# Fused two-block kernel: heads in pairs, a score group moved, a norm applied to results, a tile in another bank

## The chip, the cores and the metric

The kernel runs on one core of a Trainium2 chip. The metric is device time in microseconds (us), from the launch of the program to its end. PE is TensorE, DVE is VectorE, ACT is ScalarE, POOL is GpSimd, SP is SyncE, which issues most DMAs.

## What is computed

512 tokens of width 1024 pass two layers of a first block and one layer of a second, all in float32. Cut to what matters:

```python
for i in range(2):                                   # first block
    q_na, k_na, v_na, q_r, k_r, v_r, g_r, gate_a, gate_b = split(x @ w_in[i])
    ya = neighbourhood_attention(q_na, k_na, v_na, na_rpb[i])   # 8 heads of 64, 8x16 windows on an 8x64 grid
    yb = silu(g_r) * norm(retention(q_r, k_r, v_r))             # 4 heads, both directions
    y = (sigmoid(gate_a) * (ya @ w_branch_a) + sigmoid(gate_b) * (yb @ w_branch_b)) @ w_out[i]
    x = layer_norm(ALPHA * x + y)
    ffn = conv_glu_ffn(x); ple = sigmoid(x @ w_ple_gate) * (p[i] @ w_ple_proj)
    x = layer_norm(ALPHA * x + ffn + ple)
u = rmsnorm(h) @ w_in_2                              # second block
h = h + concat(pool_mixer(u[:, :512]), ssm_mixer(u[:, 512:])) @ w_out_2
h = h + (silu(rmsnorm(h) @ w_gate) * (rmsnorm(h) @ w_up)) @ w_down
out = rmsnorm(h)                                     # rmsnorm(x) = x / rms(x) * g
```

## The kernel before

Activations lie feature-major: `z`, `xh` and `xl` hold 8 tiles of 128 features by 512 tokens. Each float32 operand of a large product is split into a rounded part (`_hi`, float32r) and a remainder (`_lo`), and `passes` issues three products (hi*hi, lo*hi, hi*lo) in place of one.

Weights stream through a ring of four slots in *units* of 8 tiles of 128x128. SP loads a unit into `stage`, ACT rounds it to `w_hi` (L1184, `round_ahead`, three units ahead), POOL subtracts to `w_lo` (L419). PE takes a unit when `lo_done` says so. `feature_unit` runs 8 x 3 products of 512 columns into one of two unit banks, `U_BANK[0]` and `U_BANK[1]`, which alternate by the number of the result; `take_bank` waits until the reader of the result two before has freed it.

The order of each engine is written out by hand; engines meet in semaphores. One attention iteration, four in each layer, handles two neighbourhood heads and one retention head with 12 units. On PE: units 0 and 1 (q, k of the neighbourhood), 2 (v), scores and the transposes of v (`turn_v`), 3 (retention q), scores, transposes of the first probabilities (`turn_probs`), scores, 4 (retention k, the fifth unit), then probability-value products (`pv`), transposes and the two *token units* 5 and 6 in turn. A token unit writes results 5 and 6: its first half goes to bank 1, whose last reader is DVE's `rotate(0)`, its second half to bank 0, whose last reader is `rotate(1)` (L1622, L1623). Score tile i has head i // 4 and column block i % 4, lies in `S_BANK[i % 2]`, and is 256 or 384 columns wide. On DVE the order is: bias and mask of head 0 (`mask_scores(0)`, L1587, L1595, closing with the negation L1604), `normalise(0)` (L1615) behind ACT's four exps (L1214), `mask_scores(1)`, `rotate(0)`, `normalise(1)`, `rotate(1)`, then low parts for retention. The four retention score tiles (m = 0 to 3) also go through `S_BANK[m % 2]`, and DVE applies the decay (L1665).

After attention come the branches, whose merged result DVE writes at L1740, and the output projection of 8 units. For each of its results DVE runs `residual_out`: z = ALPHA*xh + result (L1751, frees the bank), z = ALPHA*xl + z (L1754); between the first and second it forms `p_lo` (L1749). POOL sums z tiles for the mean (L629).

In the mixer (second block) the output products `half_units(MS_U0...)` add to z, ACT squares each tile, POOL sums six of the squares (L629), PE forms the mean square (L947), ACT the root, DVE the reciprocal, PE spreads it over partitions (L962), and `rms` on DVE with `rms_split` on ACT writes the normed tile, its rounded part and its remainder (L1870, L1377, L1863). Only then `first_units` starts the gate and up products, whose loop handles four units a turn: ACT applies silu to the gate's bank, DVE multiplies by the up bank (`hidden`).

Of the kernel before, what the change touches and what calls it, by code (L numbers as in the profile page):

```python
# [18 lines left out]
P = 128  # L19
T = 512  # L20
# [73 lines left out]
def build(nc, a, out):  # L94

    ctx = ExitStack()
    with ctx:
# [143 lines left out]
        xn_2 = [place(f"xn_2{i}", [P, T], offset=c_at + 2048 * i) for i in range(4)]  # L241
# [4 lines left out]
        silu = [place(f"silu{i}", [P, T], offset=c_at + 2048 * i) for i in range(2)]  # L246
        hidden = [place(f"hidden{i}", [P, T], offset=c_at + 4096 + 2048 * i) for i in range(2)]
# [47 lines left out]
        z_ready, mean_done, centred = sem("z_ready"), sem("mean_done"), sem("centred")  # L295
# [25 lines left out]
        mix_hi_s, mix_lo_s = sem("mix_hi"), sem("mix_lo")  # L321
        gu_hi, gu_lo = sem("hidden_hi"), sem("hidden_lo")
# [32 lines left out]
        def _(sp):  # L355
# [53 lines left out]
            for first in range(0, KT, 2):  # L409
                sp.wait_ge(normed, (MIX * 2 + 1) * KT + (first + 2))  # L410
                sp.dma_start(out[:, first:first + 2, :], out_t[:, first:first + 2, :]).then_inc(out_done, 16)
# [4 lines left out]
        def _(pool):  # L416
# [216 lines left out]
            for L in range(DEPTH):  # L633
# [6 lines left out]
                for k in range(KT):  # L640
                    low_part(base + OUT0 // RING + 1 + k // RING, k % RING)
                    if 1 <= k < KT - 1:
                        add_tile(z_sum, z_tile, k, z_summed, 2 * L * (KT - 2), (z_ready, L * KT + (k + 1)))
# [102 lines left out]
        def _(pe):  # L746
# [28 lines left out]
            def first_units(L, u, r, x_done, ui=0, ri=0, parts=x_parts):  # L775
# [4 lines left out]
                for k in range(KT + lag):  # L780
                    for i in range(2):
# [29 lines left out]
            def attention(L, t):  # L811
# [7 lines left out]
                def scores(hh, js):  # L819
                    for r in range(2):  # L820
                        pe.wait_ge(*after_result(L, r, ri))
                    r0 = hh * NA_DH
                    q, k = ([v[r0:r0 + NA_DH, :] for v in parts] for parts in ((na_q, na_lo[0]), (na_k, na_lo[1])))
                    for j in js:
                        dst = take_score(4 * hh + j)
                        bs = kblocks(j)
                        keys = slice((j - 1 + bs[0]) * P, (j + bs[-1]) * P)
                        passes(dst[:, bs[0] * P:(bs[-1] + 1) * P], [v[:, j * P:(j + 1) * P] for v in q], [v[:, keys] for v in k],
                               True, True).then_inc(score_done, 1)
# [9 lines left out]
                def turn_probs(i):  # L839
                    j = i % CB  # L840
# [9 lines left out]
                def pv(i):  # L850
                    hh, j = i // CB, i % CB
                    if i == 0:
                        pe.wait_ge(o_norm, it * 4 + 4)
                        pe.wait_ge(v_ready, it + 1)
                    pe.wait_ge(pt_ready, it * 8 + (i + 1))
                    r0 = hh * NA_DH
                    dst = Y_BANK[r0:r0 + NA_DH, j * P:(j + 1) * P]
# [8 lines left out]
                scores(0, (0, 1))  # L866
                turn_v()
                scores(0, (2, 3))
# [11 lines left out]
                pv(2)  # L880
                pv(3)
# [3 lines left out]
                pv(4)  # L885
                pv(5)
# [3 lines left out]
                for m in range(4):  # L890
                    dst = take_score(8 + m)
# [3 lines left out]
                pv(6)  # L895
                pv(7)
# [76 lines left out]
            def out_proj(L):  # L973
# [6 lines left out]
                mean(L * 2, (z_ready, L * KT + KT))  # L980
# [58 lines left out]
            def mixer():  # L1039
# [110 lines left out]
                mean_square(n0 + 1, rstd_2, sq_2[(KT - 1) % 4])  # L1150
                spread(n0 + 1, rstd_2)
# [1136 lines left out]
```

## Time and profile before

| | us |
|---|---|
| median of 3 runs | 2444.66 |
| lowest and highest | 2443.77, 2446.43 |
| profiled execution | 2447.06 |
| its span, first to last instruction | 2445.3 |
| PE busy in it | 2366.5 (97%) |
| DVE, ACT, POOL busy | 957.5, 977.6, 1117.3 |

Times in rows count from the start of the span. A row of a timeline is a start, a duration, an engine, a line of the kernel, an operation, output and inputs with shapes, how many were merged, and in brackets the idle time of the engine ahead of it and what ended that. A PE row's duration includes the way through the array, so products overlap; their rate is read from their starts. The granted clock is a share of 2.4 GHz.

### The profile page before, as it was taken

To read this page: it belongs to the slowest core of one execution; us is meant where nothing else is said; L and a number is where in the kernel's file an instruction comes from. 1 tells how busy PE (TensorE), PEld (TensorE's weight loads), DVE (VectorE), ACT (ScalarE), POOL (GpSimd) and SP (SyncE) were. 2 spreads that over 40 slices of the span, in tenths; PEclk is the share of its full clock that TensorE was granted. 3 is DMA by queue.
4 is the path that set the end of the run, shared out by engine and by line. 5 is a ranking of instruction groups with operands and counts; after the bars stand their busy time and mean duration, and the time that the engine had idled before them with its cause. 6 is when DMAs were issued, how large, how long until landed. Compare 5 with 4: busy or idle time off the path is not lost.

```text
span 2445.3 us, 32512 instructions
## 1 busy us (share of the span) xinstructions
PE 2366.5 (97%) x11792; PEld 1947.1 (80%) x11792; DVE 957.5 (39%) x1490; ACT 977.6 (40%) x1320; POOL 1117.3 (46%) x684
## 2 busy tenths in 40 slices
PE   7999999999999998999999999999999889999998
PEld 6877888878888886888888877888887667888886
DVE  6454453343434203553553234434465594111101
ACT  4343343243555414433434225455522424444321
POOL 5677333445344453333333454344454664444442
PEclk9999999999999998999999999999999899999999
DMA  5212223213332332222222322222333112332331
GB/s 185 76 51 75 84 69 95 95 61 108 98 95 93 129 97 65 79 77 73 77 68 68 111 95 79 94 92 96 103 104 103 53 35 78 99 97 88 102 101 54
DMA packets 61136, 214.14 MB, mean 88 GB/s; under 512 B 7184, under 2 KB 7440, under 8 KB 61072
## 3 DMA queue, kind: packets, MB, share of 16 engines
q1 hardware_dynamic: 58624, 205.91, 26.3%
q10 hardware_dynamic: 2448, 7.34, 0.9%
q8 instruction: 44, 0.72, 0.1%
q14 instruction: 20, 0.16, 0.0%
HBM read 211.13 MB, written 2.10 MB: 87 GB/s over the span
## 4 chain that ended last, share of the span: by engine, by line
PE 89%; DVE 6%; ACT 2%; issue 2%; POOL 1%; SPq 0%; DMA 0%; DVEq 0%; ACTq 0%; POOLq 0%
PE psum L750 84%; PE psum L860 2%; DVE s_t L1615 1%; DVE states L1968 1%; PE psum L847 1%; ACT s_t L1214 1%; PE psum L947 1%; ACT z L1340 0%; DVE z L1762 0%; ACT xh L1339 0%; PE psum L962 0%; DMA convp<-in_convp 0%; PE psum L1063 0%; POOL rstd L629 0%; POOL w_lo L419 0%
## 5 line engine op out<-in xcount | busy, mean ns | idle before, releaser
L419 POOL TENSOR_TENSOR w_lo<-stage,w_hi 128x1024 fp32r<-128x1024 f32 x378 | 920.5, 2444 | 1261.6 <-ACT w_hi L1184 1247.0
L750 PE MATMUL psum<-xh,w_hi 128*128 128x512 f32 x1888 | 746.9, 396 | 17.5 <-DVE xl L2101 9.6
L750 PE MATMUL psum<-xl,w_hi 128*128 128x512 f32 x1888 | 741.4, 393 | 0.0
L750 PE MATMUL psum<-xh,w_lo 128*128 128x512 f32 x1888 | 741.0, 392 | 0.0
L1184 ACT ACTIVATE w_hi<-stage 128x1024 fp32r<-128x1024 f32 x377 | 396.6, 1053 | 354.0 <-PE psum L750 352.4
L750 PEld LDWEIGHTS psum<-xh,w_hi 128*128 128x128 f32 x1888 | 358.5, 190 | 100.3 <-issue 14.9
L750 PEld LDWEIGHTS psum<-xh,w_lo 128*128 128x128 f32 x1888 | 358.3, 190 | 75.9
L750 PEld LDWEIGHTS psum<-xl,w_hi 128*128 128x128 f32 x1888 | 358.8, 190 | 72.9
L750 PE MATMUL psum<-g_hi,w_hi 128*128 128x512 f32 x528 | 205.4, 389 | 0.0
L750 PE MATMUL psum<-g_lo,w_hi 128*128 128x512 f32 x528 | 205.4, 389 | 0.0
L750 PE MATMUL psum<-g_hi,w_lo 128*128 128x512 f32 x528 | 205.4, 389 | 0.0
L750 PEld LDWEIGHTS psum<-g_lo,w_hi 128*128 128x128 f32 x528 | 99.1, 188 | 20.6
L750 PEld LDWEIGHTS psum<-g_hi,w_hi 128*128 128x128 f32 x528 | 99.1, 188 | 20.6
L750 PEld LDWEIGHTS psum<-g_hi,w_lo 128*128 128x128 f32 x528 | 99.1, 188 | 20.5
L1365 ACT ACTIVATE conv_b<-psum,convp 128x512 f32<-128x512 f32 x44 | 34.3, 779 | 145.6 <-PE psum L750 145.6
L1817 DVE SCALAR_TENSOR_TENSOR conv_b<-psum,convp,conv_b 128x511 f32<-128x511 f32 x44 | 33.0, 750 | 149.3 <-ACT conv_b L1365 149.3
L2066 DVE TENSOR_TENSOR hidden<-psum,silu 128x512 f32<-128x512 f32 x22 | 15.2, 692 | 183.6 <-PE psum L750 183.6
L750 PE MATMUL psum<-w_hi,xh 128*128 128x256 f32 x256 | 74.6, 291 | 4.6 <-DVE r_tmp L1623 4.6
L750 PE MATMUL psum<-merged_p,w_hi 128*128 128x512 f32 x256 | 78.8, 389 | 0.0
L750 PE MATMUL psum<-w_lo,xh 128*128 128x256 f32 x256 | 73.1, 285 | 0.0
L750 PE MATMUL psum<-w_hi,xl 128*128 128x256 f32 x256 | 73.1, 285 | 0.0
L1839 DVE TENSOR_TENSOR z<-z,psum 128x512 f32<-128x512 f32 x16 | 11.0, 687 | 152.0 <-PE psum L750 152.0
(361 smaller groups left out, 3258.6 us busy)
## 6 DMA issues: line engine op xcount, KB each, us to landing
stage<-in_w SPq DMA_DIRECT2D x380, 512.0 KB, 3.4
bias<-in_bias ACTq DMA_DIRECT2D x8, 384.0 KB, 3.1
out_x<-out_t SPq DMA_DIRECT2D x4, 512.0 KB, 2.7
z<-in_x SPq DMA_DIRECT2D x3, 512.0 KB, 7.7
p_raw<-in_p ACTq DMA_DIRECT2D x2, 512.0 KB, 3.5
masks<-in_masks SPq DMA_DIRECT2D x1, 576.0 KB, 10.6
masks<-in_masks ACTq DMA_DIRECT2D x1, 576.0 KB, 4.6
z<-in_x SPq DMA_DIRECT2D x2, 256.0 KB, 4.4
```

The lines of the kernel that those rows point to most:

```text
L419: pool.tensor_tensor(w_lo[s][:, :, :], stage[s][:, :, :], w_hi[s][:, :, :].bitcast(F32), ALU.subtract).then_inc(lo_done, 1)
L750: mm = pe.matmul(dst, lhs[i], rhs[j], start=start and n == 0, stop=stop and n == 2)
L847: mm = pe.transpose(T_BANK[i % 2][:, b * P:(b + 1) * P], s_t[:, i, b * P:(b + 1) * P], ident[:, :])
L860: mm = pe.matmul(dst, na_v[:, j - 1 + b, r0:r0 + NA_DH], pt[:, i % 2, b * P:(b + 1) * P], start=b == bs[0], stop=b == bs[-1])
L947: mm = pe.matmul(S_BANK[1][32 * i:32 * i + 32, 0:P], mean_w[:, 0:32], tile[:, i * P:(i + 1) * P], start=first, stop=last)
L1184: act.activation(w_hi[s][:, :, :], stage[s][:, :, :], ACT.Copy).then_inc(hi_done, 1)
L1214: act.activation(s, s, ACT.Exp, bias=row_nmax[:, i:i + 1], accum_out=row_sum[:, i:i + 1])\
L1365: act.activation(buf[c][:, :], U_BANK[half][:, :], ACT.Identity, scale=convp[:, bass.ds(L, 1), 1, ch].rearrange("p l c -> p (l c)"), bias= ...
L1615: dve.tensor_scalar(s, s, row_inv[:, i:i + 1], None, ALU.mult).then_inc(p_ready, 1)
L1817: dve.scalar_tensor_tensor(out=y[:, 1:T], in0=ps[:, 0:T - 1], scalar=tap(0), in1=y[:, 1:T], op0=ALU.mult, op1=ALU.add).then_inc(conv_left, 1)
L1968: dve.tensor_tensor_scan(x[:, m, :], st[:, 4, 4 * q + m:4 * q + m + 1].to_broadcast([P, NB]), x[:, m, :], 0.0, ALU.mult, ALU.add).then_inc ...
L2066: dve.tensor_tensor(hidden[c][:, :], U_BANK[1][:, :], silu[c][:, :], ALU.mult).then_inc(bank_free[1], 1)
```

## The change

- Neighbourhood attention: score tile i now has head i % 2 and column block i // 2. `scores(j)` and `pv(j)` handle both heads of block j in turn, product by product. DVE's and ACT's helpers take a group g of four tiles (two blocks, both heads) where they took a head. Their order is as before.
- The fourth score group (block 3) stands behind unit 4 instead of ahead of it.
- The retention score tile m = 2 goes to `O_BANK`.
- `residual_out` first joins xh + xl into z for all eight tiles, `p_lo` after the second, and then needs one operation per result.
- Mixer: ACT and DVE split gain * z, without the norm, as soon as the output products have added to z. `first_units` calls the mean square ahead of its step 4 and the spread ahead of its step 8. DVE copies the scale to SBUF and multiplies each gate and up result by it; silu reads the scaled copy.

```diff
             def residual_out(L):
+                dve.wait_ge(merged_lo, L * 8 + 8)
                 for k in range(KT):
+                    dve.tensor_tensor(z[:, k, :], xh[:, k, :].bitcast(F32), xl[:, k, :].bitcast(F32), ALU.add).then_inc(z_joined, 1)
                     if k == 1:
                         dve.wait_ge(p_hi_s, L + 1)
                         stand(dve, dve_passed)
                         dve.tensor_tensor(p_lo[:, :, :], p_raw[:, :, :], p_hi[:, :, :].bitcast(F32), ALU.subtract).then_inc(p_lo_s, 1)
+                for k in range(KT):
                     unit_result(L, OUT0 + k)
-                    dve.scalar_tensor_tensor(out=z[:, k, :], in0=xh[:, k, :].bitcast(F32), scalar=ALPHA,
+                    dve.wait_ge(z_joined, L * KT + (k + 1))
+                    dve.scalar_tensor_tensor(out=z[:, k, :], in0=z[:, k, :], scalar=ALPHA,
                                              in1=U_BANK[k % 2][:, :], op0=ALU.mult, op1=ALU.add).then_inc(bank_free[k % 2], 1)
-                    dve.wait_ge(bank_free[k % 2], free_before(L, OUT_R0 + k) + 1)
-                    dve.scalar_tensor_tensor(out=z[:, k, :], in0=xl[:, k, :].bitcast(F32), scalar=ALPHA,
-                                             in1=z[:, k, :], op0=ALU.mult, op1=ALU.add).then_inc(z_ready, 1)
...
+                    for n, (a_, b_) in enumerate(((0, 0), (0, 1), (1, 0))):
+                        q, k = (na_q, na_lo[0])[a_], (na_k, na_lo[1])[b_]
+                        for hh in range(2):
+                            r0 = hh * NA_DH
+                            mm = pe.matmul(dst[hh][:, cols], q[r0:r0 + NA_DH, j * P:(j + 1) * P], k[r0:r0 + NA_DH, keys],
+                                           start=n == 0, stop=n == 2)
...
                     for b in bs:
-                        mm = pe.matmul(dst, na_v[:, j - 1 + b, r0:r0 + NA_DH], pt[:, i % 2, b * P:(b + 1) * P],
-                                       start=b == bs[0], stop=b == bs[-1])
-                    mm.then_inc(pv_done, 1)
+                        for hh in range(2):
+                            r0 = hh * NA_DH
+                            mm = pe.matmul(Y_BANK[r0:r0 + NA_DH, j * P:(j + 1) * P], na_v[:, j - 1 + b, r0:r0 + NA_DH],
+                                           pt[:, hh, b * P:(b + 1) * P], start=b == bs[0], stop=b == bs[-1])
...
-                scores(1, (0, 1))
+                scores(2)
                 turn_probs(0)
                 turn_probs(1)
-                scores(1, (2, 3))
                 feature_unit(L, 4, 4, x_parts, ui, ri)
+                scores(3)
                 pv(0)
-                pv(1)
...
-                    dst = take_score(8 + m)
+                    dst = O_BANK if m == 2 else take_score(8 + m)
...
+                def second_norm(k):
+                    if k == 4:
+                        mean_square(n0 + 1, rstd_2, sq_2[(KT - 1) % 4])
+                    if k == KT:
+                        spread(n0 + 1, rstd_2)
...
+                    act.activation(xh[:, m, :], z[:, m, :], ACT.Copy,
+                                   scale=mpar[:, NORM_C + KT + m:NORM_C + KT + m + 1]).then_inc(x_hi, 1)
...
+                def scaled_low(k):
+                    dve.wait_ge(x_hi, (n0 + 1) * KT + (k + 1))
+                    dve.scalar_tensor_tensor(out=xl[:, k, :], in0=z[:, k, :], scalar=mpar[:, NORM_C + KT + k:NORM_C + KT + k + 1],
+                                             in1=xh[:, k, :].bitcast(F32), op0=ALU.mult, op1=ALU.subtract).then_inc(x_lo, 1)
...
+                dve.tensor_copy(rms_sb[:, :], S_BANK[0][:, :]).then_inc(rms_copied, 1)
...
+                        dve.tensor_tensor(scaled[c][:, :], U_BANK[0][:, :], rms_sb[:, :], ALU.mult).then_inc(bank_free[0], 1)
...
+                        dve.tensor_tensor(hidden[c][:, :], U_BANK[1][:, :], rms_sb[:, :], ALU.mult).then_inc(bank_free[1], 1)
```

PE in attention, before: behind the first products of head 1, and after `turn_probs(0)` and `(1)` (L847), where the scores of blocks 2 and 3 follow at once.

```order
L847 MATMUL psum<-ident,s_t 128x128 [waits probs_ready]
L847 MATMUL psum<-ident,s_t 128x128 x2
L816 REGISTER_ALU [waits unit_bank_free1,unit_bank_free0]
L750 MATMUL psum<-na_k,na_q 128x384 [waits score_bank_free0]
L750 MATMUL psum<-na_k_lo,na_q 128x384
L750 MATMUL psum<-na_k,na_q_lo 128x384
L750 MATMUL psum<-na_k,na_q 128x256 [waits score_bank_free1]
L750 MATMUL psum<-na_k_lo,na_q 128x256
```

PE in attention, after: behind the last products of unit 4 (`xh`, `w_lo`), up to the first product of token unit 5.

```order
L751 MATMUL psum<-xh,w_lo_57 128x512
L818 REGISTER_ALU [waits unit_bank_free1,unit_bank_free0]
L833 MATMUL psum<-na_k,na_q 128x256 [waits score_bank_free1,score_bank_free0]
L833 MATMUL psum<-na_k,na_q 128x256
L833 MATMUL psum<-na_k_lo,na_q 128x256 x2
L833 MATMUL psum<-na_k,na_q_lo 128x256 x2
L861 REGISTER_ALU [waits ret_out_normed]
L867 MATMUL psum<-pt,na_v 64x128 [waits probs_t_ready,v_ready]
L867 MATMUL psum<-pt,na_v 64x128 x3
```

The last score products moved from behind the first transposes to behind unit 4, in pairs, each pair waiting for both score banks at once.

DVE at the start of the output projection, before: results (L1751) and remainders (L1754) in turn.

```order
L1751 SCALAR_TENSOR_TENSOR z<-xh,psum 128x512 [waits unit_used,mixer_small_params_in]
L1754 SCALAR_TENSOR_TENSOR z<-xl,z 128x512 [waits unit_bank_free0]
L1749 TENSOR_TENSOR p_lo<-p_raw,p_hi 128x1024 [waits p_hi_done]
L1751 SCALAR_TENSOR_TENSOR z<-xh,psum 128x512 [waits unit_used]
L1754 SCALAR_TENSOR_TENSOR z<-xl,z 128x512 [waits unit_bank_free1]
```

The same place after: L1752 is the join, L1760 the read of a result.

```order
L1752 TENSOR_TENSOR z<-xh,xl 128x512 [waits merged_lo,mixer_small_params_in]
L1752 TENSOR_TENSOR z<-xh,xl 128x512
L1756 TENSOR_TENSOR p_lo<-p_raw,p_hi 128x1024 [waits p_hi_done]
L1752 TENSOR_TENSOR z<-xh,xl 128x512 x6
L1760 SCALAR_TENSOR_TENSOR z<-z,psum 128x512 [waits z_joined,unit_used] x8
```

Eight joins and `p_lo` moved ahead of the first read of a result; the operation behind each result is gone.

## Rows read from the trace of the kernel before

**Rows 1.** Page, part 4: the chain that ended last, by engine.
```profile
PE 89%; DVE 6%; ACT 2%; issue 2%; POOL 1%; SPq 0%; DMA 0%; DVEq 0%; ACTq 0%; POOLq 0%
```
**Rows 2.** PE's waits, whole span: us in total, times, longest.
```profile
PE psum L750 <- DVE s_t L1587: 6.3, 8, 1.0
```
**Rows 3.** Eight stretches, unit 3 to token unit: length, busy time and count, clock, DMA.
```profile
1263.02:1277.50 14.48, 13.49 (x57) 10.63 (x57) 13.21 (x26) 5.25 (x13) 4.69 (x2) 0.76 0.19 58
...
sum 104.34, PE 94.18 PEld 74.62 DVE 94.59 ACT 45.67 POOL 58.80; mean PE 11.77 PEld 9.33 DVE 11.82 ACT 5.71 POOL 7.35
```
**Rows 4.** PE's timeline in layer 1, second iteration, unit 3 to token unit.
```profile
1075.55 0.50 PE L750 MATMUL psum<-xh,w_hi 128*128 128x512 f32 x1
...
1081.21 0.38 PE L750 MATMUL psum<-na_k,na_q 64*128 64x256 f32 x1
...
1082.29 0.77 PE L847 MATMUL psum<-ident,s_t 128*128 128x128 f32 x5
1084.04 0.44 PE L750 MATMUL psum<-na_k,na_q 64*128 64x384 f32 x1 [0.98 <-DVE s_t L1587]
...
1092.40 1.31 PE L860 MATMUL psum<-pt,na_v 128*64 128x128 f32 x10
1093.64 0.77 PE L847 MATMUL psum<-ident,s_t 128*128 128x128 f32 x5
1094.16 0.36 PE L750 MATMUL psum<-w_hi,xh 128*128 128x256 f32 x1
```
**Rows 5.** DVE's and POOL's timelines in the same iteration.
```profile
1084.86 0.56 DVE L1587 TENSOR_TENSOR s_t<-psum,bias 128x384 f32<-128x384 f32 x1
...
1087.08 0.17 DVE L1604 TENSOR_SCALAR small<-small 128x4 f32<-128x4 f32 x1
...
1090.36 3.43 DVE L1615 TENSOR_SCALAR s_t<-s_t,small 128x256 f32<-128x256 f32 x4
...
1094.55 0.69 DVE L1623 TENSOR_TENSOR r_tmp<-psum,rope 64x512 f32<-64x512 f32 x1
...
1090.60 2.39 POOL L419 TENSOR_TENSOR w_lo<-stage,w_hi 128x1024 fp32r<-128x1024 f32 x1 [7.09 <-ACT w_hi L1184]
```
**Rows 6.** Two stretches in layer 0, second iteration: the wait in token unit 5 and behind it.
```profile
148.42:153.06 4.64, 0.02 (x2) 0.00 (x1) 4.55 (x7) 0.00 (x0) 2.34 (x1) 1.00 0.56 185
153.06:157.61 4.55, 4.55 (x24) 4.42 (x25) 2.65 (x4) 0.63 (x1) 0.00 (x0) 0.62 0.15 63
```
**Rows 7.** PE's timeline in the mixer: packed products, four column groups, four row groups.
```profile
1925.38 1.95 PE L947 MATMUL psum<-sq,mean_w 128*32 128x128 f32 x64
...
1935.37 3.89 PE L1063 MATMUL psum<-u_all,w_b 32*128 32x128 f32 x64
```
**Rows 8.** PE's timeline: the third retention score tile.
```profile
1111.26 0.50 PE L750 MATMUL psum<-r_q_hi,r_k_hi 128*128 128x512 f32 x1
```
**Rows 9.** DVE's and POOL's timelines, start of layer 1's output projection.
```profile
1421.12 0.69 DVE L1740 TENSOR_TENSOR merged_p<-m_tmp,merged_p 128x512 f32 x1 [0.80 <-ACT merged_p L1298]
...
1425.03 1.56 DVE L1754 SCALAR_TENSOR_TENSOR z<-xl,z 128x512 f32<-128x512 f32 x1
1426.51 3.41 DVE L1749 TENSOR_TENSOR p_lo<-p_raw,p_hi 128x1024 fp32r<-128x1024 f32 x1
...
1423.63 5.21 POOL L419 TENSOR_TENSOR w_lo<-stage,w_hi 128x1024 fp32r<-128x1024 f32 x2 [4.56 <-ACT w_hi L1184]
1430.86 2.64 POOL L419 TENSOR_TENSOR w_lo<-stage,w_hi 128x1024 fp32r<-128x1024 f32 x1 [2.02 <-ACT w_hi L1184]
```
**Rows 10.** PE's timeline: the mean behind layer 1's output projection.
```profile
1463.77 1.13 PE L942 MATMUL psum<-z,mean_w 128*128 128x512 f32 x2 [0.59 <-DVE z L1754]
```
**Rows 11.** PE's and POOL's timelines in the mixer: from output products to gate units.
```profile
2065.38 0.43 PE L947 MATMUL psum<-rstd,mean_w 128*32 128x128 f32 x8 [2.14 <-POOL rstd L629]
...
2071.11 0.77 PE L750 MATMUL psum<-xh,w_hi 128*128 128x512 f32 x1 [2.32 <-DVE xl L1863]
...
2062.64 2.68 POOL L629 TENSOR_TENSOR rstd<-rstd,sq 128x512 f32<-128x512 f32 x2
```

More of the change, by code:

```diff
@@ L246, in build @@
         silu = [place(f"silu{i}", [P, T], offset=c_at + 2048 * i) for i in range(2)]
+        scaled = [place(f"scaled{i}", [P, T], offset=c_at + 8192 + 2048 * i) for i in range(2)]
         hidden = [place(f"hidden{i}", [P, T], offset=c_at + 4096 + 2048 * i) for i in range(2)]
@@ L409, in _ @@
             for first in range(0, KT, 2):
-                sp.wait_ge(normed, (MIX * 2 + 1) * KT + (first + 2))
+                sp.wait_ge(normed, MIX * 2 * KT + (first + 2))
                 sp.dma_start(out[:, first:first + 2, :], out_t[:, first:first + 2, :]).then_inc(out_done, 16)
@@ L817, in take_score, with scores @@
                     return S_BANK[n % 2]
-                def scores(hh, js):
+                def scores(j):
                     for r in range(2):
                         pe.wait_ge(*after_result(L, r, ri))
[L822 to L829, printed above, removed]
+                    bs = kblocks(j)
+                    cols = slice(bs[0] * P, (bs[-1] + 1) * P)
+                    keys = slice((j - 1 + bs[0]) * P, (j + bs[-1]) * P)
+                    dst = [take_score(2 * j + hh) for hh in range(2)]
+                    for n, (a_, b_) in enumerate(((0, 0), (0, 1), (1, 0))):
[4 more added lines that the diff above has]
+                                           start=n == 0, stop=n == 2)
+                            if n == 2:
+                                mm.then_inc(score_done, 1)
                 def turn_v():
@@ L1149, in mixer @@
                 half_units(MS_U0, MS_R0, 4, *ssm_mix)
-                mean_square(n0 + 1, rstd_2, sq_2[(KT - 1) % 4])
-                spread(n0 + 1, rstd_2)
-                with pe.Fori(0, FT // 2) as j:
-                    first_units(MIX, GU_U0, GU_R0, (n0 + 1) * KT, j * 4, j * 2)
-                    for m in range(2, 4):
+                def second_norm(k):
[3 more added lines that the diff above has]
+                        spread(n0 + 1, rstd_2)
+                first_units(MIX, GU_U0, GU_R0, (n0 + 1) * KT, inside=second_norm)
+                for m in range(2, 4):
+                    feature_unit(MIX, GU_U0 + m, GU_R0 + m, x_parts)
+                with pe.Fori(1, FT // 2) as j:
+                    for m in range(4):
                         feature_unit(MIX, GU_U0 + m, GU_R0 + m, x_parts, j * 4, j * 2)
@@ L1206, in ret_score_hi, with exps @@
                     act.activation(pr_hi[:, m, :], pr[m % 2][:, :], ACT.Copy).then_inc(pr_hi_s, 1)
[L1208 to L1212 removed]
+                def exps(g):
+                    act.wait_ge(nmax_ready, it * 2 + (g + 1))
+                    for i in range(4 * g, 4 * g + 4):
+                        bs = kblocks(i // 2)
                         s = s_t[:, i, bs[0] * P:(bs[-1] + 1) * P]
@@ L1372, in up @@
                                    ACT.Copy).then_inc(g_hi_s, 1)
-            def rms_split(n, tiles):
-                for k in range(KT):
-                    act.wait_ge(normed, (n - 1) * KT + (k + 1))
-                    act.activation(xh[:, k, :], tiles[k % 4][:, :], ACT.Copy).then_inc(x_hi, 1)
             def root(n, dst, ready):
```

128 lines of the change are left out of this document (58 added, 70 removed).

## Prediction

> **What bounds the kernel now.** I read the profile in this order: the page's chain of work, PE's waits, the attention loop's stretches, then the timelines of PE, DVE and POOL there. The chain is 89% PE [rows 1]: a microsecond counts only where PE issues less or waits less. In attention, PE waits once in each of the eight iterations for DVE's bias add (6.3 us in eight waits) [rows 2]. Rows 4 show one such place. Unit 3 ends at 1081.21, two score groups and five transposes run until about 1082.9, and the next scores start at 1084.04 because DVE is still scaling probabilities. That small hole costs twice: the fifth unit then needs 7.3 us (1085.1 to 1092.4) where the unit before it needed 5.66 (1075.55 to 1081.21). The stretch from the end of unit 3 to the first token unit says how often: the granted clock of its eight instances is 0.79, 1.00, 0.79, 1.00, 1.00, 0.87, 1.00 and 0.76, a mixture of the 2.4 and the 1.2 GHz level (last instance and sum in [rows 3]). The eight last 104.3 us. To this I add 6.2 us of one bank wait just behind the stretch, 4.6 us and then 24 products in 4.55 us at a mean clock of 0.62 where 2.9 would do [rows 6]. So this place costs **110.5 us** before.
>
> **Heads in pairs.** Scores (64 rows deep) and probability-value products (64 columns wide) of two heads are now issued alternately. The trace of before shows neither pair, but both kinds of packing. A probability-value pass costs 0.124 us alone (ten from 1092.40 to 1093.64) [rows 4]. Packed into four column groups, 64 passes of the same 128 columns take 1.8 us, 0.028 each; into four row groups 3.8 us, 0.060 each [rows 7]. Two column groups are half of four, so I take 0.062 per pass. Pairs 1 to 3 hold 12, 12 and 8 passes an iteration: 32 x 0.062 = 2.0 us saved, 15.8 us in eight. The bounds are no overlap (0) and 0.028 each (24.6). The first two score groups take about 2.7 us with the value transposes in between. Their 12 passes could save 1.7 us, but the second pair now wants both score banks at once and waits for DVE's two adds; I take 0.5 each time, 4 us in all, bounds 0 and 1.0. The other two pairs and the first value pair fall under the wait below and are counted there.
> The Trainium skill, "TensorE: Matmul & The Clock Gate", Part 3 (Packing small matmuls), says that a weight load overlaps a running product only where the row groups differ. The value products of both heads use the same rows. By that rule they would gain nothing and the sum would be 15.8 us higher; the four column groups at 0.028 us speak against it.
>
> **Fourth score group behind the fifth unit.** It removes the hole: two scores (about 0.6 us in a pair), four transposes (0.5) and the fifth unit at full clock (5.66) follow each other, so the group starts S = 6.8 us after unit 3. But DVE's own order is unchanged: bias and mask for all of the second half, then rotate(0), normalise(1), rotate(1). DVE now sits on the group's result, ACT's second exp sits behind DVE, and PE's first token unit needs the two unit banks that the rotates free. By rows:
> - first result at S+0.8, as 1084.04 to the add at 1084.86; four adds and masks and the negation 2.1, little less than the 2.4 up to 1087.25 [rows 5]: S+2.9.
> - bank 1 is free after two rotate products, 1.44 us: S+4.4. PE is there at about S+1.9 (scores 0.6, value pair 0.6, six transposes 0.7): it waits 2.5 us.
> - bank 0 is free 8.0 us after the negation, as 1087.25 to 1095.24 [rows 5]: S+10.9. In it normalise takes 3.43 us instead of about 1.5, since w_lo runs from 1090.60 [rows 5]; w_lo follows exp, and exp moves along. PE needs bank 0 after half a token unit (2.9 us): it waits 2 to 4 us more.
> - after a wait of that kind the clock falls, as it did behind the 4.6 us wait [rows 6]: 1.4 us of 1.65.
> From unit 3 to the point that stands for the token unit's start: 6.8 + 10.9 + 1.4 - 2.9 = 16.2 us. It was 11.3 in the full-clock instances: bank 0 came 1.9 us before its use and nobody waited. In layer 0 POOL also prepares eigenvalues, and I add 2.4 (late probabilities), 1.7 (the slow rotate of rows 6) and 3.3 us (both) to its first three instances. Sum 5 x 16.2 + 18.6 + 17.9 + 19.5 = 137.0 against 110.5: **+26.5 us**. The low end is a normalise that POOL does not block, 1.8 us less each, -14.4.
>
> **Third retention tile in O_BANK.** The third score tile starts 0.26 us after its turn (1111.26 for 1111.00) [rows 8]. That goes, but the fourth then waits for DVE's second decay product: -0.15 x 8 = -1.2 us. The bounds are 0 and -2.
>
> **Residual of the output projection.** Not in the change's name, but in its diff. DVE now joins xh and xl for all eight tiles, with p_lo among them, before it reads the first result. One DVE operation per result goes: at the end PE waited 0.59 us for it [rows 10], 1.2 us in two layers. The start is dearer. The last merged_lo ends at 1421.81. Two joins; then p_lo. DVE operations with two SBUF inputs stood while POOL ran w_lo: the add at 1425.03 took 1.56 us and p_lo 3.41, ending 1.1 us behind POOL's 1428.84 [rows 9]. With the same w_lo: p_lo from 1426.0 to 1427.1, POOL to 1429.5, three joins to 1431.3, POOL's third w_lo (1430.86 [rows 9]) to 1433.7, three joins to 1435.5, the first result read at 1436.2. PE wants that bank for the third unit at 1429.7. That is a wait of 6.4 us and 1.6 us of low clock behind it, in each layer: 16.0 - 1.2, **+14.8 us**. At the low end DVE wins the port each time and all 5.4 us of work from 1426.0 end at 1431.4: 1.7 us a layer, without a clock drop +2.2. (I take the high end: p_lo in the row lost its turn to the second w_lo.)
> The Trainium skill, "SBUF — State Buffer", section "Who interferes with whom", has the rule: a vector instruction with two SBUF inputs contends with a GpSimd instruction that reads SBUF and one of them blocks fully. The two rows agree. Before, the first operand pair held one PSUM input and was immune by that rule; the join is not.
>
> **Gate norm on results.** Before, PE ends the mixer's output products at 2063.2, waits 2.14 us for POOL's sum, then for the root and the spread, then 2.32 us for the first low part, and starts the gate units at 2071.11, ten products of them at low clock, ending at 2084.0 [rows 11]. Now xh and xl are split from the unnormed z, so 18 products (4.1 us) run at once, to 2067.4. Then the square sum needs POOL's six adds. These ended at 2065.3 [rows 11]; the eight new low parts on DVE have two SBUF inputs and push them back to about 2068. Then 0.5, 24 products (5.4), the spread (1.2) and six products (1.4): 2076.8. DVE must copy the scale and scale the first result before bank 0 is free, 1.4 us behind the spread, so no further loss. 2084.0 - 2076.8 = **-7.2 us**, bounds -5 and -8.5. In the loop DVE gains two products of 0.7 us per pair of units (10.9 us), hidden by PE.
>
> **Sum.** 26.5 - 4 - 15.8 - 1.2 + 14.8 - 7.2 = +13.1 us. The profiled execution took 2447.06 us (its span 2445.3), 2.4 above the median of the runs, 2444.66. So 2460.2 for a profiled run, **2457.8 us** as a median.
>
> **Rivals.**
> - Joins slip through (chance 0.17): the place is DVE at the start of the output projection; it decides whether DVE or POOL takes the port when p_lo ends. For it: the add at 1425.03 did win its turn. Price 12.6 us less: 2445.2, which is not slower.
> - Normalise unblocked (0.13): if the later exp shifts w_lo past the four scalings, bank 0 comes at S+9.1: 2443.4, no change. Against it: POOL's w_lo always follows exp.
> - Both together (0.13): 2430.8, faster.
> - Pairs do not overlap (0.09), so the change does not do what it says: value pairs and scores give nothing back, +19.8: 2477.6.
> - The forecast itself 0.42; the other 0.06 lie above it.
>
> **Chances and range.** What a measurement can tell from no change is 0.2%, 4.9 us. Faster than 2439.8: the double rival and 0.04 from the low edges of the single ones, 0.17. Within: the rest of the single rivals and 0.02 of the forecast, 0.28. Slower: 0.55. As cases of both signs hold much of the chance, the forecast's own range is 2450 to 2468. The range leaves out the case without overlap and half of the double rival: 2432 to 2472.
>
> **What would show each step.** In PE's waits: a new line for DVE's rotate products (L1623 of before) eight or sixteen times with some 35 us, the line for the bias add gone; a new wait on the output projection's first result of 6 us in each layer; the wait for the normed xl gone. The value passes at 0.06 us show the packing, a stretch from unit 3 to the token unit's middle of 17.7 us the bank wait. I am wrong if PE enters the token units without a wait, or if the joins end before 1430 of this clock.

## The result, and the profile after

The changed kernel takes **2497.95 us** (median of 4 runs, 2496.29 to 2500.16), the kernel before 2445.55 us beside it: a ratio of 1.0215 (95% interval 1.0197 to 1.0233), 52.4 us slower. The forecast was 2457.8 with a range up to 2472. The sign was right, the size was not: three quarters of the loss is missing from the sum. The profiled execution has a span of 2494.5 us, 49.2 more than before.

"Answers [rows N]" below names the rows of the kernel before that show the same view. The chain that ended last, by engine (answers [rows 1]), and PE's waits (us in total, times, longest; answers [rows 2]), in the changed kernel:

```profile
PE 86%; DVE 8%; ACT 2%; issue 2%; POOL 1%; SPq 0%; DMA 0%; DVEq 0%; ACTq 0%; POOLq 0%
```
```profile
PE psum L751 <- DVE r_tmp L1628: 56.4, 16, 5.4
PE psum L751 <- issue: 12.3, 2, 6.1
...
PE psum L951 <- POOL rstd L630: 0.6, 1, 0.6
PE psum L751 <- DVE scaled L2072: 0.4, 1, 0.4
```

The bias add's 6.3 us are gone, and sixteen waits of 56.4 us for DVE's rotate products stand in their place, two in each attention iteration. Two waits of 6.1 us are new; they are those of the output projection, one in a layer. The mixer's 2.1 and 2.3 us are down to 0.6 and 0.4.

The same place as [rows 4], PE in layer 1's second iteration (start, length, instruction, wait in brackets):

```profile
1113.73 0.45 PE L833 MATMUL psum<-na_k,na_q 64*128 64x384 f32 x2
...
1120.53 0.39 PE L833 MATMUL psum<-na_k,na_q 64*128 64x256 f32 x2
...
1121.08 0.66 PE L867 MATMUL psum<-pt,na_v 128*64 128x128 f32 x8
1121.67 0.87 PE L854 MATMUL psum<-ident,s_t 128*128 128x128 f32 x6
1124.89 0.55 PE L751 MATMUL psum<-w_hi,xh 128*128 128x256 f32 x1 [2.35 <-DVE r_tmp L1628]
```
```profile
1133.41 0.58 PE L751 MATMUL psum<-w_hi,xh 128*128 128x256 f32 x1 [4.02 <-DVE r_tmp L1628]
```
```profile
1138.62 0.88 PE L867 MATMUL psum<-pt,na_v 128*64 128x128 f32 x12
1139.43 0.88 PE L854 MATMUL psum<-ident,s_t 128*128 128x128 f32 x6
```

Unit 3 ends at 1113.73, and the fourth group starts at 1120.53: S = 6.80 us, as the sum had it. The hole is gone. Then PE waits for bank 1 until S+4.4, as forecast, and for bank 0 until **S+12.9**, where the sum had S+10.9. DVE, ACT and POOL in that stretch (answers [rows 5]):

```profile
1123.13 0.17 DVE L1610 TENSOR_SCALAR small<-small 128x4 f32<-128x4 f32 x1
...
1126.42 5.50 DVE L1620 TENSOR_SCALAR s_t<-s_t,small 128x384 f32<-128x384 f32 x4
...
1132.67 0.68 DVE L1628 TENSOR_TENSOR r_tmp<-psum,rope 64x512 f32<-64x512 f32 x1
```
```profile
1125.54 1.04 ACT L1195 ACTIVATE w_hi<-stage 128x1024 fp32r<-128x1024 f32 x1
...
1127.70 1.05 ACT L1195 ACTIVATE w_hi<-stage 128x1024 fp32r<-128x1024 f32 x1
```
```profile
1126.65 4.85 POOL L420 TENSOR_TENSOR w_lo<-stage,w_hi 128x1024 fp32r<-128x1024 f32 x2 [10.23 <-ACT w_hi L1195]
```

The four scalings take 5.50 us, not 3.43: POOL runs two w_lo in a row, since ACT, held back behind the second exps, now does two roundings 2.2 us apart. Bank 0 is free when the second rotate product (L1628, from 1132.67) ends. And PE's pieces in the same iteration by time, busy time and count, granted clock in the third column from the end (answers [rows 6]):

```profile
1114.87:1120.53 5.66, 5.66 (x28) 4.41 (x27) 3.18 (x5) 0.66 (x2) 1.55 (x1) 1.00 0.30 93
1124.89:1129.39 4.50, 4.50 (x24) 4.29 (x24) 4.33 (x6) 4.38 (x10) 2.74 (x2) 0.65 0.00 0
1129.39:1133.41 4.02, 0.00 (x0) 0.00 (x1) 3.93 (x5) 0.00 (x0) 2.12 (x1) 0.76 0.57 166
1133.41:1138.62 5.21, 5.21 (x24) 5.08 (x24) 2.66 (x4) 0.63 (x1) 0.00 (x0) 0.53 0.19 73
1140.06:1145.98 5.92, 5.92 (x51) 5.79 (x49) 0.00 (x0) 1.77 (x3) 2.40 (x1) 1.00 0.08 15
```

The fifth unit runs at the 2.4 GHz level. Behind the first wait 14 of the 24 products start at the pace of 1.2 GHz, behind the second 22: 4.50 and 5.21 us, where the 48 of the last row need 5.92 at full clock, so 24 need 2.96.

To compare the kernels I use one measure: the eight stretches from unit 3's end to the end of the token units, less 8 x 13.28 us, which is what the token units take in the new order without a wait (two of 5.92 us and 1.44 us of value products and transposes between them). It is the point that the prediction called the token unit's start. The stretch of layer 1's last iteration, and the sum of all eight:

```profile
1305.35:1337.45 32.10, 24.35 (x171) 21.70 (x172) 18.79 (x31) 9.75 (x22) 9.65 (x4) 0.89 0.16 51
sum 269.99, PE 208.60 PEld 185.93 DVE 155.77 ACT 82.37 POOL 115.75; mean PE 26.07 PEld 23.24 DVE 19.47 ACT 10.30 POOL 14.47
```

269.99 - 106.2 = **163.8 us**, against the 110.5 of before [rows 3, 6]: +53.3.

The output projection of layer 1, PE, DVE and POOL (answers [rows 9]):

```profile
1480.84 1.19 PE L751 MATMUL psum<-merged_p,w_hi 128*128 128x512 f32 x2 [6.15 <-issue]
```
```profile
1466.98 1.29 DVE L1752 TENSOR_TENSOR z<-xh,xl 128x512 f32<-128x512 f32 x2
1469.71 2.47 DVE L1756 TENSOR_TENSOR p_lo<-p_raw,p_hi 128x1024 fp32r<-128x1024 f32 x1 [1.44 <-ACT p_hi L1541]
1472.11 8.03 DVE L1752 TENSOR_TENSOR z<-xh,xl 128x512 f32<-128x512 f32 x6
1480.06 1.27 DVE L1760 SCALAR_TENSOR_TENSOR z<-z,psum 128x512 f32<-128x512 f32 x2
```
```profile
1468.69 5.74 POOL L420 TENSOR_TENSOR w_lo<-stage,w_hi 128x1024 fp32r<-128x1024 f32 x2 [4.56 <-ACT w_hi L1195]
1475.92 2.46 POOL L420 TENSOR_TENSOR w_lo<-stage,w_hi 128x1024 fp32r<-128x1024 f32 x1 [1.49 <-ACT w_hi L1195]
```

PE stands 6.15 us until DVE has joined all tiles and freed bank 0, much as forecast (6.4). The mixer's gate norm (answers [rows 11]):

```profile
2118.41 0.39 PE L751 MATMUL psum<-xh,w_hi 128*128 128x512 f32 x1
```
```profile
2123.21 0.43 PE L951 MATMUL psum<-rstd,mean_w 128*32 128x128 f32 x8 [0.56 <-POOL rstd L630]
```
```profile
2132.23 0.47 PE L751 MATMUL psum<-xh,w_hi 128*128 128x512 f32 x1 [0.42 <-DVE scaled L2072]
```

The output products end at 2118.4 and the first 48 gate products at 2131.6: 13.2 us, where the sum had 13.6.

### The profile page after: what moved, and what is told of

Its sections match the earlier page's. It is cut to its first block, busy times and chain, and to the rows that moved or that the text cites. A ratio compares the mean times of both kernels' runs of the same rounds, so it can differ in the third digit from the quotient of the medians.

```text
span 2494.5 us, 32602 instructions
## 1 busy us (share of the span) xinstructions
PE 2357.7 (95%) x11792; PEld 1938.2 (78%) x11792; DVE 991.6 (40%) x1527; ACT 974.6 (39%) x1320; POOL 1116.6 (45%) x684
## 4 chain that ended last, share of the span: by engine, by line
PE 86%; DVE 8%; ACT 2%; issue 2%; POOL 1%; SPq 0%; DMA 0%; DVEq 0%; ACTq 0%; POOLq 0%
PE psum L751 82%; DVE s_t L1620 2%; PE psum L867 1%; DVE states L1962 1%; PE psum L854 1%; ACT z L1350 1%; DVE z L1768 1%; PE psum L833 1%; ACT xh L1349 1%; DVE r_tmp L1628 0%; DVE r_tmp L1627 0%; PE psum L966 0%; DMA convp<-in_convp 0%; PE psum L951 0%; POOL w_lo L420 0%
## 5 line engine op out<-in xcount | busy, mean ns | idle before, releaser
L751 PE MATMUL psum<-w_hi,xh 128*128 128x256 f32 x256 | 87.3, 341 | 56.4 <-DVE r_tmp L1628 56.4
L751 PEld LDWEIGHTS psum<-g_hi,w_hi 128*128 128x128 f32 x528 | 99.1, 188 | 20.6
L751 PEld LDWEIGHTS psum<-w_hi,xh 128*128 128x128 f32 x256 | 61.6, 241 | 59.9 <-DVE r_tmp L1628 34.8
L1375 ACT ACTIVATE conv_b<-psum,convp 128x512 f32<-128x512 f32 x44 | 34.3, 780 | 144.4 <-PE psum L751 144.4
L751 PE MATMUL psum<-w_lo,xh 128*128 128x256 f32 x256 | 84.2, 329 | 0.0
L751 PE MATMUL psum<-w_hi,xl 128*128 128x256 f32 x256 | 83.7, 327 | 0.0
L1224 ACT ACTIVATE s_t<-s_t,small 128x256 f32<-128x256 f32 (+1 forms) x64 | 35.2, 551 | 96.3 <-DVE small L1610 96.3
```

The source lines that it names most:

```text
L751: mm = pe.matmul(dst, lhs[i], rhs[j], start=start and n == 0, stop=stop and n == 2)
L1224: act.activation(s, s, ACT.Exp, bias=row_nmax[:, i:i + 1], accum_out=row_sum[:, i:i + 1])\
L1375: act.activation(buf[c][:, :], U_BANK[half][:, :], ACT.Identity, scale=convp[:, bass.ds(L, 1), 1, ch].rearrange("p l c -> p (l c)"), bias= ...
```

## The experiments

The theory behind the result: the fourth group's place costs PE two bank waits per iteration, longer than forecast because of the second w_lo and of two spells of low clock; the joins cost what was forecast; the mixer gains what was forecast; the pairs work. The rival: the pairs themselves (two banks, two probability tiles wanted at once) hold PE up. Ratios below are to the kernel before, run beside each.

**The group ahead again.** The edit is on the changed kernel (in this and the next code cuts `...` marks what is left out):

```
                 turn_probs(1)
+                scores(3)
                 feature_unit(L, 4, 4, x_parts, ui, ri)
-                scores(3)
```

> The changed kernel with one line moved: the fourth score group again ahead of the fifth unit. My theory: the two bank waits in the token units (56.4 us in sixteen) and the low clock behind them come from the group's place. They go. The pair wants both score banks, so it starts some 3.8 us behind unit 3 (2.8 before the change) and leaves a longer hole there: eight stretches of 12 to 15 us to the token unit's start instead of 19 to 26, 96 to 120 us instead of 163.8. Time 2497.95 less 44 to 60 us: 2454, between 2438 and 2460. Rival, the pairs themselves hold PE up (both probabilities and both banks wanted at once): the time stays above 2485.

Measured: 2446.65 us, ratio 0.9994 (0.9984 to 1.0005); 51.3 us less than the changed kernel. Of the rotate waits one is left, that of [rows 6], and the hole is back, as PE's waits and the sum of the eight stretches show:

```profile
PE psum L833 <- DVE s_t L1593: 17.3, 8, 2.6
...
PE psum L751 <- DVE r_tmp L1628: 4.5, 1, 4.5
```
```profile
sum 224.70, PE 197.58 PEld 172.16 DVE 155.84 ACT 84.13 POOL 115.77; mean PE 24.70 PEld 21.52 DVE 19.48 ACT 10.52 POOL 14.47
```

224.7 - 106.2 = 118.5 us. The rival is out. The hole is longer than in the kernel before (17.3 us for 6.3), as the pair wants both score banks.

**The old residual.** Joins out, two operations on each result as before:

```
-                    dve.tensor_tensor(z[:, k, :], xh..., xl..., ALU.add).then_inc(z_joined, 1)
...
+                    dve.scalar_tensor_tensor(out=z[:, k, :], in0=xh..., scalar=ALPHA, in1=U_BANK[k % 2][:, :], ...)
+                    dve.scalar_tensor_tensor(out=z[:, k, :], in0=xl..., scalar=ALPHA, in1=z[:, k, :], ...)
```

> The changed kernel with the residual of the output projection as before the change: no joins ahead of the first result, two DVE operations on each. My theory: the joins and the low part of p, held up by POOL's w_lo, cost 8.85 us in layer 0 and 9.7 us in layer 1, so 18.6 us go: 2479.4. Rival, the stall is covered in part by something else that then shows (POOL's sum or the clock): only 10 to 14 us go, 2484 to 2488.

Measured: 2479.08 us, ratio 1.0134 (1.0117 to 1.0151), 18.9 us less. The two waits put down to issue are gone. So the joins cost some 17 to 19 us (16.7 by the traces of before and after, 18.9 here).

**The gate norm alone**, put into the kernel before.

> The kernel before with the gate norm on results and nothing else of the change. My theory: its 7.0 us gain in the mixer stands by itself: 2445.55 - 7.0 = 2438.5. Rival, part of it came from what the rest of the change moved ahead of the mixer: less than 5 us.

Measured: 2439.30 us beside 2447.35, ratio 0.9967 (0.9955 to 0.9978), 8.1 us less. It stands by itself.

**Values apart.** On the kernel with the group ahead:

```
-                    for b in bs:
-                        for hh in range(2):
+                    for hh in range(2):
+                        for b in bs:
```

> Run e1 with the value products of the two heads issued one head after the other, as before the change, in the same groups of 8 or 12. My theory: a pass costs 0.0675 us in a pair and 0.124 us alone, so 40 passes x 0.056 us x 8 iterations: 18 us more than e1. [...]

Measured: 2450.63 us, ratio 1.0021 (1.0011 to 1.0030), 4.0 more than with alternated heads; the ten runs of each spread over some 10 us (2445.47 to 2456.77 here, 2440.16 to 2450.07 there). The 18 us of the theory are not there. Its PE timeline, and under it that of the kernel with the group ahead:

```profile
1183.68 0.66 PE L867 MATMUL psum<-pt,na_v 128*64 128x128 f32 x8
1184.28 0.55 PE L854 MATMUL psum<-ident,s_t 128*128 128x128 f32 x3
```
```profile
1190.83 1.14 PE L867 MATMUL psum<-pt,na_v 128*64 128x128 f32 x12
1191.91 0.66 PE L854 MATMUL psum<-ident,s_t 128*128 128x128 f32 x4
```
```profile
1192.18 0.88 PE L867 MATMUL psum<-pt,na_v 128*64 128x128 f32 x12
1192.99 0.44 PE L854 MATMUL psum<-ident,s_t 128*128 128x128 f32 x2
```

From start to next start, twelve passes take 0.81 us alternated and 1.08 one head behind the other; eight take 0.60 either way (0.59 alternated in the changed kernel). Before, ten passes into one column half took 1.24 [rows 4], 0.124 each. The single products of this trace say why. In the group of twelve the first head's six start at 1190.83, 1190.99, 1191.10, 1191.21, 1191.32 and 1191.43, and the second head's first already at 1191.11, when three of the first head's have not begun. In the group of eight (four and four) the second head starts 0.01 us behind the first, again with three of the first not begun. From then on the two halves run side by side, each with a product every 0.11 us. So 4 + 4 passes need no alternating and 6 + 6 lose 0.27 us. The gain comes from both heads standing in one short group, hardly from the alternation. How far ahead the other half can start is read from groups of these two sizes alone. By these rows alternating is worth 2 x 0.27 x 8 = 4.3 us; that the medians differ by as much proves little, as the two profiled executions differ by 0.4 us only.

**Rotate(0) in DVE's gap**, between the adds of the third and the fourth group:

```
                     for i in range(4 * g + 1, 4 * g + 4):
+                        if g == 1 and i == 6:
+                            dve.wait_ge(cos_sin_in, L * 16 + 16)
+                            rotate(0, r_q)
                         add_bias(i)
...
-                rotate(0, r_q)
                 normalise(1)
```

> The changed kernel with rotate(0) put on DVE between the adds of the third and of the fourth score group, where DVE stood idle for 3.1 us. My theory: with S the start of the fourth group, bank 1 is free long before S+1.9, so PE's first wait of 2.35 us goes, and bank 0 comes at S+8.1 to S+10 instead of S+12.9, as rotate(0) no longer stands behind the negation. PE's wait for bank 0 stays, 3 to 5 us, and with it the low clock behind. 2.9 to 4.8 us in eight places: 2497.95 less 23 to 38: 2460 to 2475. Rival, bank 0 is set by ACT's exp and POOL's w_lo alone and comes as late as before: no more than 5 us go.

Measured: 2469.10 us, ratio 1.0097 (1.0077 to 1.0118), 28.9 less, inside the forecast. PE's first wait is gone, the second is longer (49.3 us in eight), and bank 0 comes at S+10.1: in layer 1's second iteration the second rotate's products end at 1116.55, and S is 1106.4. But most of the 2.7 us by which bank 0 is earlier have another cause than the theory's:

```profile
1111.74 3.37 DVE L1623 TENSOR_SCALAR s_t<-s_t,small 128x384 f32<-128x384 f32 x4
```
```profile
1112.52 4.79 POOL L420 TENSOR_TENSOR w_lo<-stage,w_hi 128x1024 fp32r<-128x1024 f32 x2 [10.22 <-ACT w_hi L1195]
```

Without rotate(0) in the way the scalings start only 0.55 us sooner after S, because DVE then waits for ACT's exps. They take 3.37 us instead of 5.50, though POOL again runs two w_lo in a row: the first w_lo starts 0.78 us behind the first scaling (0.24 in the changed kernel), when three of the four scalings have begun, and only the last one stands (2.44 us).

**One w_lo fewer on the scaling:**

```
-                round_ahead(L, 5, ui)
                 for k, x in enumerate((r_q, r_k)):
                     ...
+                round_ahead(L, 5, ui)
```

> The changed kernel with ACT's rounding of the weights of unit 8 (round_ahead(5)) behind the two copies of the rotated parts, so that POOL has one w_lo, not two in a row, while DVE scales the probabilities. My theory: the second w_lo is what makes the scaling 5.50 us instead of 3.43 and bank 0 2.05 us later than I predicted. 2.05 x 8 = 16 us go: 2482 (2479 to 2485). Rival, PE takes it back by the clock, or the scaling is held by something else: less than 5 us.

Measured: 2467.46 us, ratio 1.0090 (1.0070 to 1.0111): 30.5 us less, twice the forecast. DVE and POOL in the same iteration, and below them the same two in the next kernel, in which three w_lo come together:

```profile
1111.89 3.39 DVE L1620 TENSOR_SCALAR s_t<-s_t,small 128x384 f32<-128x384 f32 x4
```
```profile
1112.13 2.41 POOL L420 TENSOR_TENSOR w_lo<-stage,w_hi 128x1024 fp32r<-128x1024 f32 x1 [10.23 <-ACT w_hi L1195]
```
```profile
1080.40 7.70 DVE L1623 TENSOR_SCALAR s_t<-s_t,small 128x384 f32<-128x384 f32 x4
```
```profile
1080.64 7.32 POOL L420 TENSOR_TENSOR w_lo<-stage,w_hi 128x1024 fp32r<-128x1024 f32 x3 [10.23 <-ACT w_hi L1195]
```

Four scalings that meet one, two or three w_lo: 3.39, 5.50, 7.70 us. Singly they take 0.34 to 0.42 us, and 2.4 to 2.6 when a w_lo runs first (0.42, 2.56, 2.42 and 0.34 in the changed kernel): DVE and POOL take turns, one scaling to one w_lo. Bank 0 comes 2.1 us earlier; PE's rotate waits fall from 56.4 to 42.4 us, and PE is busy for 6.6 us less, at a higher clock: together the 20.6 us by which the eight stretches are shorter (163.8 to 143.2). The other 8 to 10 us lie outside these stretches: from the end of layer 1's attention to the end of the span the changed kernel took 1124.2 us, this one 1116.5, others with the same code there 1118.3 to 1121.6. It is so in the other runs too: of the 51.3 us of the group ahead 45.3 lie in the eight stretches, of the 28.9 us of rotate(0) in the gap 21.9. One wait in the mixer (for DVE's t_s) is 7.0 us in some traces (the changed kernel's among them) and 3.8 in others (this one's among them). What sets it is open; a difference of 4 us between two of these kernels says nothing about attention.

**Both rotates early.** Besides the gap edit:

```
-                exps(1)
-                round_ahead(L, 4, ui)
                 copy_out(4, r_k[:, :])
+                exps(1)
+                round_ahead(L, 4, ui)
...
+                rotate(1, r_k)
                 normalise(1)
-                rotate(1, r_k)
```

> Run e5 and besides the copy of unit 4's result ahead of ACT's second exps, the rounding of the next weights behind them, and rotate(1) ahead of the second scaling on DVE. My theory: both banks are free before PE asks (bank 0 at S+4.3, PE at S+4.9), no wait and full clock: unit 3 to the point that stands for the token unit's start takes 8.7 us instead of 19 to 26, in layer 0 up to 3 us more: 163.8 becomes 70 to 82. 2497.95 less 82 to 94: 2404 to 2416. Rival, the probabilities come too late (transposes wait for the scaling, value products for ACT's copies): 2430 to 2450.

Measured: **2412.70 us**, ratio 0.9862 (0.9843 to 0.9881), 85.3 less than the changed kernel and faster than the one before. Layer 1's second iteration:

```profile
1067.72:1089.65 21.93, 21.93 (x171) 19.66 (x172) 20.92 (x31) 9.76 (x22) 9.73 (x4) 1.00 0.26 75
```

PE is busy in every microsecond of it, at full clock; the scaling's 7.70 us are waited for by nobody. The eight make 193.4 - 106.2 = 87.2 us, not 70 to 82: layer 0's first three still wait for late probabilities and a bank (26.1, 26.4 and 31.3 us). POOL prepares eigenvalues there, up to 48 operations in a stretch instead of 4; that this is the cause was not tested. 76.6 of the 85.3 us lie in the eight stretches.

**The group ahead, both rotates early.** It asks whether the group's new place is worth anything.

> Run e7 with the fourth score group ahead of the fifth unit again. My theory: the group behind the unit does remove the hole ahead of it (13.8 us of stretch becomes 8.6 in layer 1), if the rotates are early. With the group ahead the hole and its low clock are back: as run e1, 2444 to 2447, 32 us more than e7. Rival, the whole gain of e7 over e1 is in the rotates: 2410 to 2420.

Measured: 2439.85 us, ratio 0.9968 (0.9954 to 0.9981), 27 us more than with the group behind the unit. So both halves are needed: the group's move alone loses 51, the rotates' alone gain 7, together they gain 34, each against the kernel with the group ahead. The 7 is more than I expected; it is layer 0's bank wait that goes, the one of [rows 6] (that stretch falls from 34.3 to 25.9 us).

**The joins spread:** two ahead of the first result, then one behind each:

```
+                join(0)
+                join(1)
                 for k in range(KT):
+                    if k == 2:
+                        ... p_lo ...
                     unit_result(L, OUT0 + k)
                     ...
+                    if k + 2 < KT:
+                        join(k + 2)
```

> The changed kernel with the joins of the residual spread: two ahead of the first result, then one behind each result for the tile after the next, the low part of p behind the second result. My theory: the stall at the start of the output projection goes and the end keeps its gain: 18.6 us and perhaps 1 more: 2478.5 (2476 to 2481). Rival, a join that POOL's w_lo holds up delays a bank: 2482 to 2488.

Measured: 2476.99 us, ratio 1.0127 (1.0107 to 1.0148), 21.0 less. From the branches' start to the first product of p the layer takes 127.7 us (changed 137.0, before 128.7): 9.3 a layer, 18.6 in two, as the theory had it. The other 2.4 us lie elsewhere; the mixer's wait is 3.8 in this trace and 7.0 in the changed kernel's. The joins' idea was good, 1.0 us a layer against before; their place was not.

**Only the low part of p later** (behind the third result, all joins still ahead of the first):

> The changed kernel with the low part of p taken out of the joins and put behind the third result. My theory: DVE's work ahead of the first result shrinks by p_lo (2.47 us in the trace), and what is left is eight joins of 0.6 us held up by one or two w_lo of 2.4: PE's wait of 6.1 us becomes 2 to 4, in each layer, with a little less low clock behind it: 5 to 10 us go, 2488 to 2493. Rival, POOL's two w_lo set the end of the joins whatever DVE has to do: less than 2 us go.

Measured: 2483.64 us, ratio 1.0155 (1.0140 to 1.0171): 14.3 us less, more than forecast. PE, DVE and POOL there:

```profile
1473.86 0.70 PE L751 MATMUL psum<-merged_p,w_hi 128*128 128x512 f32 x2 [2.31 <-issue]
```
```profile
1463.84 9.32 DVE L1752 TENSOR_TENSOR z<-xh,xl 128x512 f32<-128x512 f32 x8
```
```profile
1465.55 5.25 POOL L420 TENSOR_TENSOR w_lo<-stage,w_hi 128x1024 fp32r<-128x1024 f32 x2 [4.57 <-ACT w_hi L1195]
```

DVE's work before the first result now takes 9.3 us, where it was 13.1 (1466.98 to 1480.06). The wait falls by 3.8, and behind the wait of 2.3 us the twelve next products take 2.84 us instead of 5.25. The layer is 6.7 us shorter (130.3 for 137.0), 13.4 in two. The theory's "a little less low clock" was too small; POOL does not set the end alone.

**All of it**, with and without the w_lo edit:

> Runs e6, e7 and e8 in one: both rotates early, the joins spread, and unit 8's rounding behind the rotated parts. My theory: the gains of e7 and e8 lie in different places and add up: 2412.7 less 18.6 to 21 us is 2393; of e6's edit only layer 0 can gain, where PE still waits 3.3 us for the scaling in the third iteration, so 2388 to 2393. Rival, with the attention shorter the weights or POOL's w_lo come late: above 2398.

> Runs e7 and e8 in one, without e6's edit. My theory: 2393 (2391 to 2396), as three w_lo in a row make the second scaling 7.7 us but nobody waits for it in layer 1. Rival as for the run with e6's edit.

Measured: **2396.02 us**, ratio 0.9795 (0.9781 to 0.9809), and 2397.75 us, ratio 0.9806 (0.9791 to 0.9821). The gains of "both rotates early" and "the joins spread" add up to 2412.7 - 21.0 = 2391.7; the measured times are 4 and 6 us above it, both outside what I expected. Most of that can be placed: only 18.6 of the joins' 21.0 us lie at the output projection, and the mixer's wait is 3.8 us in the traces of those two and 7.0 in both of these. 2412.7 - 18.6 + 3.2 = 2397.3. The w_lo edit can't be told from nothing by the runs (1.7 us between the medians, inside their spread); the two traces have it where it was expected, in layer 0: with it the first three stretches take 26.1, 25.3 and 27.9 us, without it 26.1, 26.4 and 31.4. The first is 50.7 us faster than the kernel before (2446.75 beside it), and 102 faster than the changed one.

## Why the prediction was right or wrong, step by step

| term | predicted | measured |
| --- | --- | --- |
| fourth group behind the unit | +26.5 | +53.3 |
| first two score groups | -4 | -3.5 |
| value pairs | -15.8 | -12.1 |
| third retention tile | -1.2 | 0 |
| residual | +14.8 | +16.7 (traces), +18.9 (run) |
| gate norm | -7.2 | -7.0 (trace), -8.1 (run) |

The measured column is from the two traces, between the same points of PE's order in both; it sums to 47.4 of the 49.2 us between the spans. The run of the old residual and that of the gate norm alone give the second figures.

- **The step that failed is bank 0, "8.0 us behind the negation".** It was 10.05. I carried over normalise's 3.43 us with one w_lo from [rows 5], and wrote that w_lo follows exp and moves along. I did not ask what else ACT has queued behind the exps. Before, two w_lo stood 5.4 us apart (1090.60 and the row below); in the new order ACT runs its roundings for units 7 and 8 2.2 us apart, and POOL blocks DVE twice. The run with one w_lo fewer shows the 2.1 us. The Trainium skill, "SBUF — State Buffer", section "Who interferes with whom", says that a tensor_scalar in a two-port mode and a GpSimd instruction exclude each other fully; 3.39, 5.50 and 7.70 us agree. The trace of before also held the long case, which I passed over as a "slow rotate": at the bank wait of [rows 6], in layer 0's second iteration, the scalings took 5.29 us beside three w_lo in a row.

```profile
1096.01 2.40 POOL L419 TENSOR_TENSOR w_lo<-stage,w_hi 128x1024 fp32r<-128x1024 f32 x1 [3.02 <-ACT w_hi L1184]
```
```profile
146.27 5.29 DVE L1615 TENSOR_SCALAR s_t<-s_t,small 128x256 f32<-128x256 f32 x4
```
```profile
142.79 7.97 POOL L419 TENSOR_TENSOR w_lo<-stage,w_hi 128x1024 fp32r<-128x1024 f32 x3
```

- **The clock behind the wait.** I took 1.4 us from [rows 6], where 24 products took 4.55 us. Here there are two waits in a row, and the 24 behind the second take 5.21: 2.3 us above the 2.96 at full clock. With S+12.9 this gives 6.8 + 12.9 + 2.3 - 2.96 = 19.0 us for a normal instance against 16.2; the five measured are 18.8 to 19.2. That is 14 us of the 26.8 missed.
- **Layer 0's three instances** are the other 13: 22.3, 20.9 and 25.7 us, where I had 18.6, 17.9 and 19.5. Of these, 3 x 2.8 = 8.4 us are the same two errors as in a normal instance. So bank 0 and the clock behind it make 22 of the 26.8 us missed. The remaining 4.5 us are in what I added on top for layer 0, mostly in the third: there PE waits 2.8 us for probabilities and then 4.5 us, not 2.35, for bank 1. Why bank 1 comes later there was not tested.
- **Right in the same term:** S = 6.8 us, the hole's end, full clock in the fifth unit, bank 1 at S+4.4 and the wait of 2.35 us. The rival "normalise unblocked" was the mirror of the truth, and no case of mine had a longer scaling, though the trace of before had one; the upper end of the range, with the pairs' rival as its only step up, was too near for that reason.
- **Value pairs.** A pass costs 0.0675 us (0.81 for twelve), near the 0.062. But three groups of 12, 12 and 8 now replace three of ten: 3.72 - 2.21 = 1.51 us an iteration, 12.1 in eight, not 2.0 and 15.8; I had multiplied the passes of after by the saving of one. The rival by the skill's packing rule is out: pairs overlap though their rows are the same.
- **Third retention tile.** The gap moved on whole, as these starts show; the fourth tile starts 0.26 us after its turn (1149.36):

```profile
1148.67 0.40 PE L751 MATMUL psum<-r_q_hi,r_k_hi 128*128 128x512 f32 x1
...
1149.62 0.50 PE L751 MATMUL psum<-r_q_hi,r_k_hi 128*128 128x512 f32 x1
```

- **Residual.** The wait (6.15 for 6.4) came as listed, and so did the order: two joins, p_lo between the first and the second w_lo, three joins, the third w_lo, three joins. The clock behind took 2.5 us, not 1.6: twelve products in 5.25 us. The rival "joins slip through" is out.
- **Gate norm.** Right in each part: PE starts on POOL's sum 4.8 us behind the output products, as forecast (0.56 us of it a wait), and no loss of note at the first result.

## What to carry to other kernels

Moving PE's work to fill a hole moves whoever waits for its result; the move pays only if the other engines' queues are put in the new order too (51 us lost without it, 34 gained with it). When a step slides behind a later event on an in-order engine, list everything queued behind it there and what that will set off together: two operations of the same kind that were apart before can arrive as one block. If a trace of before has a slow instance of the step, ask what made it slow and whether the change makes that the rule. Work that is merely not needed yet, like the joins, belongs between results and not ahead of the first.

## What the runs showed of the hardware that I had not expected

- Short products into two column halves of the array (the same rows) run side by side if both halves stand in a short group, in whichever order: eight passes 0.59 to 0.60 us, twelve 0.81 or 1.08, ten into one half 1.24. The Trainium skill, "TensorE: Matmul & The Clock Gate", Part 3 (Packing small matmuls), lets a weight load overlap a running product only in other row groups; here both halves use all 128 rows and start their products in pairs, so the measurement decides against that for column halves.
- A wait of 2.35 us already leaves the next 24 products at a clock of 0.65, and another of 4.02 us the 24 behind it at 0.53, close to pure 1.2 GHz: together 3.8 us more than at 2.4 GHz. At the output projection a wait of 2.31 us cost next to nothing (the next twelve products 2.84 us) where one of 6.15 us cost 2.5 (5.25 us).
- DVE scalings (0.34 to 0.42 us each) and w_lo on POOL (2.4 us) take turns one by one. Each w_lo that gets its turn before the last of four scalings costs them 2.1 to 2.2 us: 3.39, 5.50 and 7.70 us with one, two and three. Two in a row cost no more than one (3.37 us) when the first starts 0.78 us behind the first scaling.
